# Feed-forward up projections: the high weights over both input halves as one matmul of 512 columns

## The chip, the cores and the metric

The kernel runs on one core of one Trainium2 chip. The metric is the device time of one execution in microseconds (us). The kernel before has a median of 1065.12 us over three runs (1064.92 to 1067.35).

## The reference

Three layers over 256 tokens of width 1024. The first two each have an attention mixer and, behind it, a feed-forward part; the third is a hybrid layer that the change doesn't touch. Everything is float32. The feed-forward part is:

```python
def conv_ffn(x, w_up, conv_w, conv_b, w_down):
    u = x @ w_up                                  # 1024 -> 2 * 2816
    up = jnp.pad(u, ((0, 0), (1, 1), (0, 0)))
    c = conv_b
    for j in range(3):
        c = c + conv_w[j] * up[:, j:j + s]        # three taps along the tokens
    g, val = c[..., :2816], c[..., 2816:]
    return (jax.nn.gelu(g) * val) @ w_down        # 2816 -> 1024
```

## The kernel before

**Products in two halves.** A float32 product is made of three matmuls in the type fp32r: each operand is split into a high half (a copy rounded to fp32r) and a low half (the value less the high half), and high x high, high x low and low x high are summed in PSUM (`mm3`, L397: L399 is weights high by input high, L400 weights high by input low, L401 weights low by input high). The input's halves are `xh` and `xl`, each eight blocks of 128 channels by 256 tokens. The weights come in chunks of 128 x 1024 into six slots `raw[0]` to `raw[5]`. ScalarE (ACT) makes `high` from `raw` (`split_high`, L357), and VectorE (DVE) or GpSimd (POOL) makes `low` (`split_low`, L368). In the feed-forward part GpSimd makes slot 3's and VectorE the others'. SyncE issues the load of the next chunk as soon as the slot's `low` is done.

**The feed-forward part** has 11 steps in each of two layers. A step has two halves, j = 0 and 1. A half takes 128 hidden channels: an up projection for the gate (slot and PSUM bank 2j) and one for the value (slot and bank 2j+1), each by `project_t` over eight blocks with three matmuls of 256 columns (24 matmuls), written to `W[bank][:, 0:TOK]` with TOK = 256; the other 256 columns of the bank are not used here. The down projection (slot 4+j) is 12 matmuls of 512 columns into `acc`. TensorE's order in a step (`ffn_pe`) is up(0, i), down(1, i-1), up(1, i), down(0, i); in the last step down(1, i-1) stands behind up(1, i).

**Between them**, for each half: ScalarE computes the middle tap and the bias of the gate from PSUM into `cg` (L1071), VectorE adds the two outer taps (L1118, L1121), the same for the value into `cv`, ScalarE applies GELU (L1077), GpSimd multiplies (`h`, L1156; the trace calls `h32` h), ScalarE copies the product's high half (`hh`, L1083) and GpSimd makes the low half (`hl`, L1158). Down needs both.

**What sets the order.** Each engine runs one hand-written list in order, and waits on semaphores in it. Per half ScalarE's list is: cg, high of the gate's slot, cv, high of the value's slot, GELU, (wait for h) hh, then one more high: slot 5 behind half 0, slot 4 behind half 1. VectorE's is: two taps on cg, low of the gate's slot, two taps on cv, low of the value's slot (GpSimd's for slot 3), with slot 5's low between the halves and slot 4's behind half 1. GpSimd's is: h, hl for half 0; h, hl, low of slot 3 for half 1. The first and the last step are written out, the nine between them are a loop. In the last step the highs and lows of half 1's slots stand later.

Of the kernel before, what the change touches and what calls it, by code (L numbers as in the profile page):

```python
# [23 lines left out]
P = 128  # L24
# [234 lines left out]
def build(nc, dram, y_out):  # L259
# [5 lines left out]
    def sb(name, shape, dt=F32):  # L265
        return scope[-1].enter_context(nc.sbuf_tensor(name, shape, dt))
# [28 lines left out]
    hid = sb("hid", [P, NT, D])  # L295
    hn = sb("hn", [P, NT, D])
    junk = sb("junk", [P, 512])
    xh = sb("xh", [P, KB, TOK], F32R)
    xl = sb("xl", [P, KB, TOK], F32R)
    stat = sb("stat", [P, 24])  # L300
    mean = sb("mean", [P, 16])

# [106 lines left out]
    def project_t(pe, out, k, width=P, offset=0, x=None, blocks=KB, arriving=None):  # L409


        x = x or (xh, xl)
        for b in range(blocks):
            if arriving is not None and b % 4 == 0:
                pe.wait_ge(n_["xl"], 4 * arriving + 2 + b // 2)
            o = b * width + offset
            last = mm3(pe, out, wslot(k, o, o + P), (x[0][:, b, :], x[1][:, b, :]), b == 0, b == blocks - 1)
        return last
# [602 lines left out]
    def ffn_pe(pe, layer):  # L1021
        p = (ph["ffn0"], ph["ffn1"])[layer]
        done = layer * FFN_STEPS

        def up(j, i):

            for gate, bank in ((1, 2 * j), (0, 2 * j + 1)):
                chunk_ready(pe, p, bank, i)
                if not (isinstance(i, int) and i + done == 0):
                    pe.wait_ge(f[j]["g_tap"] if gate else f[j]["v_tap"], 2 * (i + done))  # L1030
                first = isinstance(i, int) and i == 0 and j == 0 and gate
                project_t(pe, W[bank][:, 0:TOK], bank, arriving=2 * layer + 1 if first else None).then_inc(used[bank], 1)

        def down(j, i, start=False, stop=False):

            chunk_ready(pe, p, 4 + j, i)
            pe.wait_ge(f[j]["hl"], i + done + 1)
            rows_out(pe, 4 + j, hh[j], hl[j], start, stop).then_inc(used[4 + j], 1)

        def step(i):  # L1040
            last_step = isinstance(i, int) and i == FFN_STEPS - 1
            up(0, i)
            if not (isinstance(i, int) and i == 0) and not last_step:
                down(1, i - 1)
            up(1, i)
            if last_step:
                down(1, i - 1)
            down(0, i, start=isinstance(i, int) and i == 0)

        over(pe, FFN_STEPS, step)  # L1050
        seen = FFN_STEPS + done
        rows_out_end(pe, p, 5, 5, hh[1], hl[1], (f[1]["hh"], seen), (f[1]["hl"], seen))
# [6 lines left out]
    def ffn_act(act, layer):  # L1059
        p = (ph["ffn0"], ph["ffn1"])[layer]  # L1060
        done = layer * FFN_STEPS
        split = hi_of(act)

        def block(j, i, between):
            late = j == 1 and isinstance(i, int) and i == FFN_STEPS - 1
            for value in range(2):
                bank, s = 2 * j + value, f[j]
                act.wait_ge(used[bank], p.base[bank] + i + 1)
                if value and not (isinstance(i, int) and i + done == 0):
                    act.wait_ge(s["h32"], i + done)  # L1070
                act.activation((cg, cv)[value][j][:], W[bank][:, 0:TOK], ACT.Identity,  # L1071
                               scale=ffn_taps(layer, i, j, value, 1, 0),
                               bias=ffn_taps(layer, i, j, value, 3, 0)).then_inc((s["g_mid"], s["v_mid"])[value], 1)
                if not late:
                    refill(split, p, bank, i)
            act.wait_ge(f[j]["g_tap"], 2 * (i + done) + 2)
            act.activation(gelu[j][:], cg[j][:], ACT.Gelu_apprx_tanh).then_inc(f[j]["gelu"], 1)  # L1077
            if late:
                refill(split, p, 5, i - 1)
            act.wait_ge(f[j]["h32"], i + done + 1)  # L1080
            if not (isinstance(i, int) and i + done == 0):
                act.wait_ge(used[4 + j], used_before(i, j))
            act.activation(hh[j][:], h32[j][:], ACT.Copy).then_inc(f[j]["hh"], 1)  # L1083
            if late:
                for bank in (2 * j, 2 * j + 1):
                    refill(split, p, bank, i)
            between()

        def used_before(i, j):
            return p.base[4 + j] + i  # L1090

        def after_first(i):
            if not isinstance(i, int):
                refill(split, p, 5, i - 1)
            elif i == 0 and layer == 0:
                split(p, 5, 0)

        def step(i):
            if isinstance(i, int) and i == FFN_STEPS - 1:
                first_of_next(split, p)  # L1100
            block(0, i, lambda: after_first(i))
            block(1, i, lambda: refill(split, p, 4, i))

        over(act, FFN_STEPS, step)
        refill(split, p, 5, FFN_STEPS - 1)

    def ffn_dve(dve, layer):
        p = (ph["ffn0"], ph["ffn1"])[layer]
        done = layer * FFN_STEPS
        split = lo_of(dve)  # L1110

        def block(j, i):
            last_step = isinstance(i, int) and i == FFN_STEPS - 1
            for value in range(2):
                bank, s = 2 * j + value, f[j]
                mid, tap, c = (s["g_mid"], s["v_mid"])[value], (s["g_tap"], s["v_tap"])[value], (cg, cv)[value][j]
                dve.wait_ge(mid, i + done + 1)
                dve.scalar_tensor_tensor(c[:, 1:TOK], W[bank][:, 0:TOK - 1], ffn_taps(layer, i, j, value, 0, 0),  # L1118
                                         c[:, 1:TOK], ALU.mult, ALU.add).then_inc(tap, 1)
                dve.wait_ge(tap, 2 * (i + done) + 1)  # L1120
                dve.scalar_tensor_tensor(c[:, 0:TOK - 1], W[bank][:, 1:TOK], ffn_taps(layer, i, j, value, 2, 0),  # L1121
                                         c[:, 0:TOK - 1], ALU.mult, ALU.add).then_inc(tap, 1)
                if not (j and last_step):
                    refill(split, p, bank, i)

        def step(i):
            last_step = isinstance(i, int) and i == FFN_STEPS - 1
            block(0, i)
            if not isinstance(i, int):
                refill(split, p, 5, i - 1)  # L1130
            block(1, i)
            if isinstance(i, int) and i == 0:
                split(p, 5, 0)
            if last_step:
                refill(split, p, 5, i - 1)
                for bank in (2, 3):
                    refill(split, p, bank, i)
                first_of_next(split, p)
            if not (last_step and layer):
                refill(split, p, 4, i)  # L1140

        over(dve, FFN_STEPS, step)
        refill(split, p, 5, FFN_STEPS - 1)

    def ffn_pool(pool, layer):
        p = (ph["ffn0"], ph["ffn1"])[layer]
        done = layer * FFN_STEPS
        split = lo_of(pool, True)

        def hidden(j, i):  # L1150
            s = f[j]
            pool.wait_ge(s["gelu"], i + done + 1)
            pool.wait_ge(s["v_tap"], 2 * (i + done) + 2)
            if not (isinstance(i, int) and i + done == 0):
                pool.wait_ge(s["hh"], i + done)
            pool.tensor_tensor(h32[j][:], gelu[j][:], cv[j][:], ALU.mult).then_inc(s["h32"], 1)  # L1156
            pool.wait_ge(s["hh"], i + done + 1)
            pool.tensor_tensor(hl[j][:], h32[j][:], hh[j][:], ALU.subtract).then_inc(s["hl"], 1)  # L1158

        def step(i):  # L1160
            hidden(0, i)
            if not (isinstance(i, int) and i == 0):
                refill(split, p, 5, i - 1)
            refill(split, p, 0, i)
            refill(split, p, 1, i)
            hidden(1, i)
            refill(split, p, 2, i)
            refill(split, p, 3, i)
            refill(split, p, 4, i)
            if isinstance(i, int) and i == FFN_STEPS - 1:  # L1170
                first_of_next(split, p)

        over(pool, FFN_STEPS, step)
        refill(split, p, 5, FFN_STEPS - 1)
# [1514 lines left out]
    def att_pool(pool):  # L2689
# [14 lines left out]
        with pool.Fori(2, HEADS - 2) as r:  # L2704
# [3 lines left out]

    r_ = dict(tha=f[0]["g_mid"], thb=f[0]["v_mid"], mh=f[0]["hh"], ma=f[0]["g_tap"], mb=f[0]["v_tap"],
              sum=f[1]["g_tap"], ml=f[1]["v_tap"])  # L2710
    ACT_SEEN, DVE_SEEN = 2 * FFN_STEPS, 4 * FFN_STEPS
    tha, thb = sb("tha", [P, TOK]), sb("thb", [P, TOK])
    mga, mgb = sb("mga", [P, TOK]), sb("mgb", [P, TOK])
    mg = sb("mg", [P, TOK])
# [291 lines left out]
```

## Time and profile before

| | |
|---|---|
| median of three runs | 1065.12 us |
| the profiled execution's own time | 1066.56 us |
| its span, first to last instruction | 1064.8 us |
| mean granted TensorE clock | 0.997 |
| busy: TensorE / weight loads / VectorE / ScalarE / GpSimd | 1036.0 / 950.1 / 663.6 / 560.7 / 417.6 us |
| feed-forward part of layer 0, of layer 1 | about 128 to 312 us, 453 to 637 us |

The time around the span is 1.8 us. The matmuls of `mm3` are pipelined: a row shows each with its whole latency, so that the rows overlap, and what one costs is the distance between starts. Shares of busy time are averages over all stages; the feed-forward parts together are about a third of the span, and the sections below look at them alone.

### The profile page before, as it was taken

The page shows a single profiled execution, that of the slowest core. Times are in us where ns is not written, and L with a number is a line of the kernel's source. Part 1 is how long each engine was busy: PE and PEld are TensorE (multiplying, and loading weights), DVE is VectorE, ACT ScalarE, POOL GpSimd, SP SyncE. Part 2 cuts the span into 40 slices and gives each one's busy share as a digit, 9 for nine tenths or more (in the row PEclk, how much of TensorE's full clock was granted, in tenths as well). Part 3 has the DMA queues.
Part 4 walks back from the last instruction along what each step waited for, and adds up shares of the span by engine and source line. Part 5 has one row for each costly group of instructions (what it writes and reads, how often), then busy time and mean ns, then how long its engine had stood idle before and what let it go on. Part 6 is the DMA issues. An engine that isn't in the chain of part 4 may idle for free.

```text
span 1064.8 us, 21773 instructions
## 1 busy us (share of the span) xinstructions
PE 1036.0 (97%) x8216; PEld 950.1 (89%) x8216; DVE 663.6 (62%) x1074; ACT 560.7 (53%) x1022; POOL 417.6 (39%) x283
## 2 busy tenths in 40 slices
PE   9899999999999999999999999999999999999997
PEld 7799699999978998699999987899999899999996
DVE  4555767677665665776766755766676555554545
ACT  4555665555555555756555565644443355554433
POOL 1000234433351334334333463865653365534431
PEclk9999999999999999999999999999999999999999
DMA  8333465665543443365656434333213245546551
GB/s 317 120 124 128 132 218 186 195 197 178 177 159 130 140 147 131 114 225 183 205 184 201 159 102 148 110 120 109 92 61 120 80 133 149 155 137 209 199 181 43
DMA packets 46136, 162.27 MB, mean 152 GB/s; under 512 B 5248, under 2 KB 5504, under 8 KB 45952
## 3 DMA queue, kind: packets, MB, share of 16 engines
q1 hardware_dynamic: 44784, 156.78, 45.1%
q0 software_dynamic: 1296, 4.72, 1.4%
q8 instruction: 38, 0.62, 0.2%
q14 instruction: 18, 0.15, 0.0%
HBM read 160.43 MB, written 1.05 MB: 152 GB/s over the span
## 4 chain that ended last, share of the span: by engine, by line
PE 90%; DVE 3%; POOL 3%; ACT 2%; issue 1%; DMA 1%; DVEq 0%; SPq 0%; ACTq 0%
PE work L399 14%; PE work L401 14%; PE work L400 14%; PE work L1688 9%; PE acc L399 6%; PE acc L400 6%; PE acc L401 6%; PE work L2410 4%; PE work L2422 2%; PE acc L2422 2%; POOL low L368 1%; PE acc L1939 1%; PE acc L1953 1%; PE acc L1955 1%; POOL stat L559 1%
## 5 line engine op out<-in xcount | busy, mean ns | idle before, releaser
L368 POOL TENSOR_TENSOR low<-raw,high 128x1024 fp32r<-128x1024 f32 x109 | 265.7, 2441 | 293.4 <-ACT high L357 290.9
L368 DVE TENSOR_TENSOR low<-raw,high 128x1024 fp32r<-128x1024 f32 (+2 forms) x184 | 273.2, 1493 | 159.3 <-ACT high L357 159.2
L357 ACT ACTIVATE high<-raw 128x1024 fp32r<-128x1024 f32 (+2 forms) x293 | 299.5, 1032 | 43.9 <-DMA raw<-in_w_out 29.1
L399 PE MATMUL work<-xh,high 128*128 128x256 f32 (+1 forms) x1032 | 290.0, 281 | 0.7 <-DVE low L368 0.7
L400 PE MATMUL work<-xl,high 128*128 128x256 f32 (+1 forms) x1032 | 287.9, 279 | 0.0
L401 PE MATMUL work<-xh,low 128*128 128x256 f32 (+1 forms) x1032 | 287.8, 279 | 0.0
L399 PEld LDWEIGHTS work<-xh,high 128*128 128x128 f32 (+1 forms) x1032 | 193.2, 187 | 7.6 <-issue 4.8
L400 PEld LDWEIGHTS work<-xl,high 128*128 128x128 f32 (+1 forms) x1032 | 193.3, 187 | 2.0 <-issue 0.3
L401 PEld LDWEIGHTS work<-xh,low 128*128 128x128 f32 (+1 forms) x1032 | 193.3, 187 | 0.2
L1156 POOL TENSOR_TENSOR h<-gelu,cv 128x256 f32<-128x256 f32 x44 | 50.5, 1149 | 198.7 <-ACT gelu L1077 102.0
L1688 PE MATMUL work<-xh,high 128*128 128x256 f32 x256 | 76.7, 300 | 0.0
L1688 PE MATMUL work<-xl,high 128*128 128x256 f32 x256 | 71.7, 280 | 0.0
L1688 PE MATMUL work<-xh,low 128*128 128x256 f32 x256 | 71.4, 279 | 0.0
L399 PE MATMUL acc<-high,hh 128*128 128x512 f32 x168 | 65.9, 392 | 0.0
L400 PE MATMUL acc<-low,hh 128*128 128x512 f32 x168 | 65.8, 392 | 0.0
L401 PE MATMUL acc<-high,hl 128*128 128x512 f32 x168 | 65.4, 389 | 0.0
L1083 ACT ACTIVATE hh<-h 128x256 fp32r<-128x256 f32 x44 | 18.4, 418 | 77.7 <-POOL h L1156 77.7
L1688 PEld LDWEIGHTS work<-xh,high 128*128 128x128 f32 x256 | 48.1, 188 | 2.5
L1071 ACT ACTIVATE cv<-work,vec 128x256 f32<-128x256 f32 x44 | 24.8, 565 | 47.4 <-PE work L401 47.4
L1688 PEld LDWEIGHTS work<-xl,high 128*128 128x128 f32 x256 | 48.2, 188 | 0.0
L1688 PEld LDWEIGHTS work<-xh,low 128*128 128x128 f32 x256 | 48.1, 188 | 0.0
L1158 POOL TENSOR_TENSOR hl<-h,hh 128x256 fp32r<-128x256 f32 x44 | 34.1, 776 | 24.4 <-ACT hh L1083 24.4
(385 smaller groups left out, 2201.2 us busy)
## 6 DMA issues: line engine op xcount, KB each, us to landing
raw<-in_w_ffn SPq DMA_DIRECT2D x132, 512.0 KB, 4.3
raw<-in_w_out SPq DMA_DIRECT2D x39, 512.0 KB, 4.5
raw<-in_w_att SPq DMA_DIRECT2D x32, 512.0 KB, 3.7
raw<-in_w_diff SPq DMA_DIRECT2D x31, 512.0 KB, 4.3
raw<-in_w_gdn SPq DMA_DIRECT2D x24, 512.0 KB, 4.0
raw<-in_w_mla SPq DMA_DIRECT2D x8, 512.0 KB, 3.6
raw<-in_w_gdnz SPq DMA_DIRECT2D x8, 512.0 KB, 3.6
raw<-in_w_mla SPq DMA_DIRECT2D x8, 384.0 KB, 3.1
```

What stands on the lines that cost most here:

```text
L357: act.activation(high[k][:, 0:w], raw[k][:, 0:w], ACT.Copy).then_inc(high_done[k], 1)
L368: eng.tensor_tensor(low[k][:, 0:w], raw[k][:, 0:w], high[k][:, 0:w], ALU.subtract).then_inc(low_done[k], 1)
L399: pe.matmul(out, lhs[0], rhs[0], start=start, stop=False)
L400: pe.matmul(out, lhs[0], rhs[1], start=False, stop=False)
L401: return pe.matmul(out, lhs[1], rhs[0], start=False, stop=stop)
L1071: act.activation((cg, cv)[value][j][:], W[bank][:, 0:TOK], ACT.Identity, scale=ffn_taps(layer, i, j, value, 1, 0), bias=ffn_taps(layer, i, ...
L1083: act.activation(hh[j][:], h32[j][:], ACT.Copy).then_inc(f[j]["hh"], 1)
L1156: pool.tensor_tensor(h32[j][:], gelu[j][:], cv[j][:], ALU.mult).then_inc(s["h32"], 1)
L1158: pool.tensor_tensor(hl[j][:], h32[j][:], hh[j][:], ALU.subtract).then_inc(s["hl"], 1)
L1688: last = pe.matmul(W[x][:, 0:TOK], l[slot][:, b * P:(b + 1) * P], r[:, b, :], start=(s == 0), stop=(s == 23))
L2410: last = pe.matmul(W[0][:, t * TOK:(t + 1) * TOK], x[:, b, t * P:(t + 1) * P], w[k][:, o:o + TOK], start=(b == 0 and term == 0), stop=(b = ...
L2422: last = pe.matmul(out, w[k][:, b * P:(b + 1) * P], x[:, b, :], start=(s == 0), stop=(s == 23))
```

## The change

In the up projections the matmuls "weights high by input high" and "weights high by input low" become one matmul of 512 columns. Its moving operand is a view over both input halves, which now lie in one tensor, and it writes both halves of the PSUM bank: the first 256 columns hold high x high, to which the matmul of low weights still adds, and the last 256 hold high x low. So a block has two matmuls instead of three. The two sums are then added outside TensorE: ScalarE copies the second sum to SBUF (into `gelu` for the gate, `h32` for the value, which are free at that time) and VectorE adds it to the first in PSUM. Only then ScalarE computes the middle tap. The semaphores `g_tap` and `v_tap` count four events a step instead of two: copy, sum, and the two taps. Mixers, down projections and the hybrid layer keep their three matmuls.

```diff
-    xh = sb("xh", [P, KB, TOK], F32R)
-    xl = sb("xl", [P, KB, TOK], F32R)
+    x_both = sb("x_both", [P, 2, KB, TOK], F32R)
+    xh, xl = x_both[:, 0, :, :], x_both[:, 1, :, :]
...
+        def project_wide(bank, arriving):
+            out, both = W[bank][:, 0:TOK], W[bank][:].rearrange("p (a k) -> p a k", a=2)
+            for b in range(KB):
+                if arriving is not None and b % 4 == 0:
+                    pe.wait_ge(n_["xl"], 4 * arriving + 2 + b // 2)
+                h_, l_ = wslot(bank, b * P, (b + 1) * P)
+                if b == KB - 1:
+                    pe.matmul(out, l_, xh[:, b, :], start=False, stop=False)
+                last = pe.matmul(both, h_, x_both[:, :, b, :], start=(b == 0), stop=(b == KB - 1))
+                if b < KB - 1:
+                    pe.matmul(out, l_, xh[:, b, :], start=False, stop=False)
+            return last
...
-                    pe.wait_ge(f[j]["g_tap"] if gate else f[j]["v_tap"], 2 * (i + done))
+                    pe.wait_ge(f[j]["g_tap"] if gate else f[j]["v_tap"], 4 * (i + done))
-                project_t(pe, W[bank][:, 0:TOK], bank, arriving=2 * layer + 1 if first else None).then_inc(used[bank], 1)
+                project_wide(bank, 2 * layer + 1 if first else None).then_inc(used[bank], 1)
...
                 act.wait_ge(used[bank], p.base[bank] + i + 1)
+                if not (isinstance(i, int) and i + done == 0):
+                    act.wait_ge(s["hl"] if value else s["h32"], i + done)
+                act.activation((gelu, h32)[value][j][:], W[bank][:, TOK:2 * TOK],
+                               ACT.Copy).then_inc((s["g_tap"], s["v_tap"])[value], 1)
+                act.wait_ge((s["g_tap"], s["v_tap"])[value], 4 * (i + done) + 2)
...
-            act.wait_ge(f[j]["g_tap"], 2 * (i + done) + 2)
+            act.wait_ge(f[j]["g_tap"], 4 * (i + done) + 4)
...
+                dve.wait_ge(tap, 4 * (i + done) + 1)
+                dve.tensor_tensor(W[bank][:, 0:TOK], W[bank][:, 0:TOK], (gelu, h32)[value][j][:], ALU.add).then_inc(tap, 1)
                 dve.wait_ge(mid, i + done + 1)
...
-                dve.wait_ge(tap, 2 * (i + done) + 1)
+                dve.wait_ge(tap, 4 * (i + done) + 3)
...
-            pool.wait_ge(s["v_tap"], 2 * (i + done) + 2)
+            pool.wait_ge(s["v_tap"], 4 * (i + done) + 4)
```

The hybrid layer reuses these semaphores; the count from which it starts is raised to match.

## Rows read from the trace of the kernel before

**Rows 1.** The page, part 1: busy time of each engine, with its share and count

```profile
PE 1036.0 (97%) x8216; PEld 950.1 (89%) x8216; DVE 663.6 (62%) x1074; ACT 560.7 (53%) x1022; POOL 417.6 (39%) x283
```

**Rows 2.** Timeline of PE in one step: start us, us, what

```profile
209.25 0.28 PE L399 MATMUL work<-xh,high 128*128 128x256 f32 x1
...
214.86 0.39 PE L399 MATMUL acc<-high,hh 128*128 128x512 f32 x1
...
217.60 0.28 PE L399 MATMUL work<-xh,high 128*128 128x256 f32 x1
```

**Rows 3.** What PE waited for, longest in total: us, times, longest us

```profile
PE work L515 <- DVE hn L547: 4.3, 6, 1.9
```

**Rows 4.** Timeline of ACT, one round from hh to hh

```profile
161.29 0.42 ACT L1083 ACTIVATE hh<-h 128x256 fp32r<-128x256 f32 x1 [2.23 <-POOL h L1156]
161.62 1.04 ACT L357 ACTIVATE high<-raw 128x1024 fp32r<-128x1024 f32 x1
162.56 0.55 ACT L1071 ACTIVATE cg<-work,vec 128x256 f32<-128x256 f32 x1
163.01 1.05 ACT L357 ACTIVATE high<-raw 128x1024 fp32r<-128x1024 f32 x1
...
170.90 0.42 ACT L1083 ACTIVATE hh<-h 128x256 fp32r<-128x256 f32 x1 [3.46 <-POOL h L1156]
...
177.61 0.42 ACT L1083 ACTIVATE hh<-h 128x256 fp32r<-128x256 f32 x1 [2.23 <-POOL h L1156]
```

**Rows 5.** Timeline of DVE, the same round

```profile
162.69 3.28 DVE L368 TENSOR_TENSOR low<-raw,high 128x1024 fp32r<-128x1024 f32 x1 [2.31 <-ACT high L357]
165.89 0.47 DVE L1118 SCALAR_TENSOR_TENSOR cg<-work,vec,cg 128x255 f32<-128x255 f32 x1
166.51 0.48 DVE L1121 SCALAR_TENSOR_TENSOR cg<-work,vec,cg 128x255 f32<-128x255 f32 x1
166.91 1.21 DVE L368 TENSOR_TENSOR low<-raw,high 128x1024 fp32r<-128x1024 f32 x1
168.04 0.47 DVE L1118 SCALAR_TENSOR_TENSOR cv<-work,vec,cv 128x255 f32<-128x255 f32 x1
...
169.06 1.22 DVE L368 TENSOR_TENSOR low<-raw,high 128x1024 fp32r<-128x1024 f32 x1
172.30 1.23 DVE L368 TENSOR_TENSOR low<-raw,high 128x1024 fp32r<-128x1024 f32 x1 [2.03 <-ACT high L357]
...
176.22 0.48 DVE L1121 SCALAR_TENSOR_TENSOR cv<-work,vec,cv 128x255 f32<-128x255 f32 x1
```

**Rows 6.** Timeline of POOL, the same round

```profile
162.49 2.40 POOL L368 TENSOR_TENSOR low<-raw,high 128x1024 fp32r<-128x1024 f32 x1
169.22 1.65 POOL L1156 TENSOR_TENSOR h<-gelu,cv 128x256 f32<-128x256 f32 x1 [4.33 <-DVE cv L1121]
...
176.84 0.73 POOL L1156 TENSOR_TENSOR h<-gelu,cv 128x256 f32<-128x256 f32 x1 [4.70 <-issue]
```

**Rows 7.** Timeline of ACT: hh of half 1 in steps 0, 8, 9 of layer 0

```profile
144.94 0.42 ACT L1083 ACTIVATE hh<-h 128x256 fp32r<-128x256 f32 x1 [2.22 <-POOL h L1156]
...
276.35 0.42 ACT L1083 ACTIVATE hh<-h 128x256 fp32r<-128x256 f32 x1 [0.91 <-POOL h L1156]
...
293.04 0.42 ACT L1083 ACTIVATE hh<-h 128x256 fp32r<-128x256 f32 x1 [0.90 <-POOL h L1156]
```

**Rows 8.** The same in steps 0 and 9 of layer 1

```profile
469.00 0.42 ACT L1083 ACTIVATE hh<-h 128x256 fp32r<-128x256 f32 x1 [2.22 <-POOL h L1156]
...
618.04 0.42 ACT L1083 ACTIVATE hh<-h 128x256 fp32r<-128x256 f32 x1 [0.90 <-POOL h L1156]
```

**Rows 9.** Groups of DVE by line and form: busy us, mean ns, idle before

```profile
L1898 DVE TENSOR_TENSOR work<-work,const 64x256 f32<-64x256 f32 x8 | 3.5, 434 | 1.4 <-ACT mt L1815 1.3
```

**Rows 10.** Timeline of POOL: the first scalar step behind each layer's feed-forward part

```profile
313.07 0.56 POOL L601 TENSOR_TENSOR stat<-mean,vec 128x1 f32<-128x1 f32 x1
...
639.42 0.56 POOL L601 TENSOR_TENSOR stat<-mean,vec 128x1 f32<-128x1 f32 x1
```

More of the change, by code:

```diff
@@ L2710, in build @@
               sum=f[1]["g_tap"], ml=f[1]["v_tap"])
-    ACT_SEEN, DVE_SEEN = 2 * FFN_STEPS, 4 * FFN_STEPS
+    ACT_SEEN, DVE_SEEN = 2 * FFN_STEPS, 8 * FFN_STEPS
     tha, thb = sb("tha", [P, TOK]), sb("thb", [P, TOK])
```

## The prediction

> **What bounds the kernel now.** I read the page's busy times first, then TensorE's starts inside one feed-forward step, then what TensorE waited for, and last the lists of the other three engines over one step. TensorE is busy 97% of the span and VectorE 62%, ScalarE 53%, GpSimd 39% [rows 1]. That alone says that TensorE's work is the time, and that the rest has room. Both hold only on average, so the feed-forward step has to be read for itself.
>
> *TensorE's step.* Between 209.25 and 214.86 lie two up projections, 48 matmuls of 256 columns: 5.61 us, 0.117 us each. Between 214.86 and 217.60 lies one down projection, 12 of 512 columns: 2.74 us, 0.228 us each [rows 2]. A step has two of either: 2 x (5.61 + 2.74) = 16.70 us. Inside the feed-forward parts TensorE waits for nobody: its longest waits of all are for `hn`, between the parts, 1.9 us at most [rows 3].
>
> *The round of the other engines.* This is the view that decides. In the second and third step they do not wait for TensorE, because they are a little late, so their list shows its own length. From `hh` of half 1 at 161.29 to the next at 177.61 the round takes 16.32 us [rows 4], only 0.38 us less than TensorE's step. Followed piece by piece, one engine works and the others wait: ScalarE's hh and high of slot 4; VectorE's low of slot 4 from 162.69, which lasts 3.28 us and not 1.22 because GpSimd's low of slot 3 started at 162.49 and ran until 164.89 [rows 5, 6]; then taps (165.89, 166.51), low (166.91), taps (168.04), low (169.06); GpSimd's h at 169.22, whose 1.65 us again lies partly behind VectorE's low; hh at 170.90, a high, VectorE's low (172.30), taps, low, taps until 176.70; h at 176.84; hh at 177.61 [rows 4 to 6]. VectorE's tap follows its own previous low at once: the middle tap `cg` was computed by ScalarE long before, at 162.56, while VectorE was in its low [rows 4, 5]. Later in the part the round has caught up and TensorE sets the pace: hh at 276.35 and 293.04, 16.69 us apart [rows 7]. So two loops of nearly equal length run side by side.
>
> **The change, part by part.**
>
> *TensorE.* A block had 3 x 0.117 = 0.351 us and gets 0.228 + 0.117 = 0.345 us, at the pace of [rows 2]; one matmul of 512 columns is hardly shorter than two of 256. With 32 blocks a step that is 16.52 us, 0.18 less; over 22 steps 3.9 us. This is all that the change can bring. (For the 512-column matmul over two separate regions of SBUF there is no row. If the second region cost nothing it is the above; if it cost as much as the two matmuls that it replaces, the gain is zero.)
>
> *ScalarE's copy.* 88 copies of 128x256 from PSUM. The nearest row is `cg` itself, 0.55 us [rows 4]. It goes in front of `cg`, where ScalarE waits for TensorE or VectorE anyway. While VectorE does taps and a low (over 2 us), ScalarE does one high of 1.05 us [rows 4], then the next copy. I cost the copies at nothing. Their cover is VectorE's list; without it each would cost 0.4 to 0.55 us.
>
> *VectorE's add, and the two waits.* Here is the price. VectorE's list for a bank was: tap, tap, low. It becomes: add, wait for `cg`, tap, tap, low. `cg` may only start when the add is done, so it can no longer be computed behind VectorE's previous low: VectorE stands still while ScalarE computes it, and what is queued behind it, the taps and the low of the next chunk, moves by as much. A round trip per bank costs
> - the add: 0.43 us (256 columns from PSUM and SBUF to PSUM: [rows 9]; the taps with 255 columns take 0.47 [rows 5]);
> - VectorE to ScalarE: 0.04 us, as GpSimd to ScalarE (h ends at 176.84 + 0.73 = 177.57, hh starts at 177.61 [rows 4, 6]);
> - `cg`: 0.56 us [rows 4];
> - ScalarE back to VectorE: 0.04 us.
>
> Together 1.07 us, four times a step: 4.28 us. None of it has cover, since [rows 4 to 6] show that every piece of the round waits for the one before. GELU adds 0.05 us: ScalarE reaches it behind high, about when the taps end. The rest of the round keeps its shape: the low of slot 3 on GpSimd still starts 0.2 us ahead of slot 4's on VectorE, and hits it as before; the new adds meet no work of GpSimd. The round becomes 16.32 + 4.28 + 0.05 = 20.65 us.
>
> So TensorE, with 16.52 us of work, is no longer the bound. It will wait in each step: laid out from these numbers, about 3.5 us for `hl` of half 0 in front of down(0), 0.6 us in front of down(1). The loads gain room, and I cost them at nothing: they are issued when a low is done, and a step is 4 us longer.
>
> For the add alone the Trainium skill has a price (VectorE: DVE Perf Modes, "The TRN2 errata"): with a PSUM source 120 cycles and one per element at 0.96 GHz, here 0.39 us. By it the sum would be about 3 us lower; the row above goes by what was measured here.
>
> *The sum.* From hh of half 1 in step 0 to that in step 9 there are nine rounds: 9 x 20.65 = 185.9 us. Before it was 293.04 - 144.94 = 148.1 us in layer 0 [rows 7] and 618.04 - 469.00 = 149.0 us in layer 1 [rows 8]. That is +37.8 and +36.9. The first step: two round trips lie fully behind each other, of the first two a part lies behind TensorE; laid out in the same way, hh of half 1 comes 3.3 us later in layer 0 and 3.6 us in layer 1. The last step: four round trips (4.3 us), less what the engines had waited for TensorE there. I follow it to GpSimd's first scalar step of the norm, at 313.07 and 639.42 [rows 10], which waits for GpSimd's last low and not for TensorE: +1.8 and +2.8 us. All together 37.8 + 36.9 + 3.3 + 3.6 + 1.8 + 2.8 = 86 us. The profiled execution took 1066.56 us, 1.4 us above the median of 1065.12; against it 1152.8, against the median **1151 us**.
>
> *The bounds.* Round trip: with the shortest add and `cg` that these rows allow (0.38 and 0.50) and no handing over it is 0.9 us; with 0.47 for the add and 0.1 us more at each hand-over, since in the loop two dependent taps start 0.62 us apart although one takes 0.47 [rows 5], it is 1.3 us. Over 88 banks that is 15 us less or 20 us more. Hence 1136 to 1171 within this case.
>
> **The rivals.**
>
> *TensorE stays the bound: faster.* If the round has slack that I don't see, for instance because `cg` lets VectorE go on with the next low first, the four round trips vanish and only TensorE's 3.9 us are left: 1061 us. The point at which it decides is the length of the round: it must stay under 16.52 us, and before it had 16.32, so only 0.2 us is free for four round trips. For it speaks the average load of VectorE and ScalarE [rows 1]; against it that the hand-written list puts the wait ahead of taps and low. Chance 0.04.
>
> *Half-hidden: no change.* The round trips cost just what the 0.38 us of slack and TensorE's gain hold, about 0.15 us each, if add and `cg` ran nearly side by side. Time 1062 to 1068. The waits forbid it. Chance 0.03.
>
> *TensorE's clock falls.* The granted clock was full, with waits of at most 1.9 us [rows 3]; the new wait of 3.5 us in each step is longer than any of them. If the clock fell to the lower level behind every such wait and stayed there, TensorE's step would take twice 16.52 us, 33 us, against a round of 20.65: 22 x 12.4 = 270 us more, some 1420 us. If it only stayed for a few microseconds, TensorE would lose less than the 4 us that it waits anyway, and the time stays. Chance of the bad form 0.05.
> The Trainium skill says that idleness brings the clock down (TensorE: Matmul & The Clock Gate, Part 1: the array runs at 1.2 GHz by default and activity releases it to 2.4 GHz). No row here has it lowered inside a feed-forward part.
>
> *The collision moves away.* If VectorE's low of slot 4 came ahead of GpSimd's low of slot 3, it would take 1.22 instead of 3.28 us and the round 18.6 us: about 1108 us. The order hangs on 0.2 us [rows 5, 6], but both start from the same `hh`. Chance 0.04.
>
> **How the numbers follow.** The likeliest case, a round of about 20.65 us, has 0.84. The range of 8 in 10 cuts its thin ends: 1138 to 1169 us. What a measurement of this kernel can tell from no change is 0.3%, 3 us. Faster by more than that: 0.04; within it: 0.03; slower: 0.93.
>
> **What would show it.** Right: hh of half 1 lies 20 to 21.3 us apart in both layers; VectorE idles about 0.65 us in front of each first tap, released by `cg`; TensorE waits for `hl` in each step, longest near 3.5 us, and its busy share falls to about 90%; pairs of matmuls start 0.345 us apart; the chain that ended last runs through add, cg, tap and low and no longer through matmuls alone. Wrong: a distance of 16.5 us between those `hh`, the copies rather than the adds on the chain, or a granted clock well under 0.99.

## The result, and the profile after

The kernel with the change takes 1170.13 us (median of four runs, 1169.61 to 1170.45) against 1065.69 us before: a ratio of 1.0977, with a 95% interval of 1.0958 to 1.0996. It is slower, as forecast, but by 104 us and not by 86: the time lies 1 us above the range of 1138 to 1169.

The page after, parts 1 and 2 of the changed kernel (against [rows 1]):

```profile
PE 1075.9 (92%) x7512; PEld 943.0 (81%) x7512; DVE 699.6 (60%) x1162; ACT 586.8 (50%) x1110; POOL 413.1 (35%) x283
...
PEclk9999989898899999999888899899999999999999
```

TensorE's busy time has grown, although 704 matmuls are gone, and the granted clock has dips in the two feed-forward parts. ScalarE and VectorE have got 26 and 36 us more work, in 103 us more span, so their busy shares have even fallen. Part 4 of the page gives the chain of work that ended last. Before, it was nearly all TensorE:

```profile
PE 90%; DVE 3%; POOL 3%; ACT 2%; issue 1%; DMA 1%; DVEq 0%; SPq 0%; ACTq 0%
```

In the changed kernel it is a mixture:

```profile
PE 53%; DVE 15%; ACT 13%; issue 11%; POOL 6%; ACTq 1%; DVEq 1%; POOLq 0%
ACT high L357 8%; PE work L1709 8%; DVE low L368 7%; PE work L399 6%; PE work L401 5%; PE work L400 5%; POOL h L1177 4%; PE work L2431 4%; DVE work L1137 3%; PE work L2443 2%; PE acc L399 2%; PE acc L401 2%; PE acc L400 2%; ACT cg L1090 2%; DVE cg L1139 2%
```

The round of the other engines, seen as in [rows 4 to 6], one round after the change. ScalarE:

```profile
213.52 0.42 ACT L1102 ACTIVATE hh<-h 128x256 fp32r<-128x256 f32 x1 [0.90 <-POOL h L1177]
...
218.79 0.56 ACT L1090 ACTIVATE cg<-work,vec 128x256 f32<-128x256 f32 x1 [3.63 <-DVE work L1137]
...
222.28 0.56 ACT L1090 ACTIVATE cv<-work,vec 128x256 f32<-128x256 f32 x1 [1.71 <-DVE work L1137]
...
229.07 0.56 ACT L1090 ACTIVATE cg<-work,vec 128x256 f32<-128x256 f32 x1 [1.60 <-DVE work L1137]
...
232.54 0.57 ACT L1090 ACTIVATE cv<-work,vec 128x256 f32<-128x256 f32 x1 [1.69 <-DVE work L1137]
...
235.27 0.42 ACT L1102 ACTIVATE hh<-h 128x256 fp32r<-128x256 f32 x1 [0.90 <-POOL h L1177]
```

VectorE in the same round:

```profile
214.93 3.28 DVE L368 TENSOR_TENSOR low<-raw,high 128x1024 fp32r<-128x1024 f32 x1 [2.31 <-ACT high L357]
218.13 0.42 DVE L1137 TENSOR_TENSOR work<-work,gelu 128x256 f32<-128x256 f32 x1
219.52 0.48 DVE L1139 SCALAR_TENSOR_TENSOR cg<-work,vec,cg 128x255 f32<-128x255 f32 x1 [0.97 <-ACT cg L1090]
...
221.68 0.42 DVE L1137 TENSOR_TENSOR work<-work,h 128x256 f32<-128x256 f32 x1
222.99 0.48 DVE L1139 SCALAR_TENSOR_TENSOR cv<-work,vec,cv 128x255 f32<-128x255 f32 x1 [0.89 <-ACT cv L1090]
...
227.24 1.23 DVE L368 TENSOR_TENSOR low<-raw,high 128x1024 fp32r<-128x1024 f32 x1 [2.01 <-ACT high L357]
228.38 0.43 DVE L1137 TENSOR_TENSOR work<-work,gelu 128x256 f32<-128x256 f32 x1
229.78 0.48 DVE L1139 SCALAR_TENSOR_TENSOR cg<-work,vec,cg 128x255 f32<-128x255 f32 x1 [0.98 <-ACT cg L1090]
...
231.94 0.42 DVE L1137 TENSOR_TENSOR work<-work,h 128x256 f32<-128x256 f32 x1
233.25 0.48 DVE L1139 SCALAR_TENSOR_TENSOR cv<-work,vec,cv 128x255 f32<-128x255 f32 x1 [0.89 <-ACT cv L1090]
```

And GpSimd:

```profile
214.72 2.41 POOL L368 TENSOR_TENSOR low<-raw,high 128x1024 fp32r<-128x1024 f32 x1
224.33 1.48 POOL L1177 TENSOR_TENSOR h<-gelu,cv 128x256 f32<-128x256 f32 x1 [7.21 <-DVE cv L1142]
...
234.49 0.74 POOL L1177 TENSOR_TENSOR h<-gelu,cv 128x256 f32<-128x256 f32 x1 [7.43 <-ACT gelu L1096]
```

From hh at 213.52 to the next at 235.27 the round takes 21.75 us; it was 16.32. In front of each first tap VectorE now stands idle for 0.89 to 0.98 us "<-ACT cg" or cv, and ScalarE in front of each of its own for 1.6 to 3.6 us "<-DVE work": each waits for the other. VectorE's low of 3.28 us next to GpSimd's of 2.41 is as before.

What TensorE waited for in the changed kernel (us in total, times, longest), against [rows 3]:

```profile
PE acc L399 <- POOL hl L1179: 60.7, 23, 3.8
```

In the looped steps this is one wait a step, in front of down(0); the forecast second one, of 0.6 us in front of down(1), doesn't appear. Behind the wait TensorE drops in most steps for a few microseconds to the lower of its two clock levels, 1.2 instead of 2.4 GHz: the matmuls of the down projection then start 0.43 us apart and not 0.23.

```profile
227.21 0.47 PE L399 MATMUL acc<-high,hh 128*128 128x512 f32 x1 [1.98 <-POOL hl L1179]
...
229.89 0.63 PE L399 MATMUL acc<-high,hh 128*128 128x512 f32 x1
230.32 0.63 PE L400 MATMUL acc<-low,hh 128*128 128x512 f32 x1
```

### The profile page after: what moved, and what is told of

It is laid out like the page before. It is cut to its first block, busy times and chain, and to the rows that moved or that the text cites. A ratio compares the mean times of both kernels' runs of the same rounds, so it can differ in the third digit from the quotient of the medians.

```text
span 1168.2 us, 20661 instructions
## 1 busy us (share of the span) xinstructions
PE 1075.9 (92%) x7512; PEld 943.0 (81%) x7512; DVE 699.6 (60%) x1162; ACT 586.8 (50%) x1110; POOL 413.1 (35%) x283
## 3 DMA queue, kind: packets, MB, share of 16 engines
HBM read 160.43 MB, written 1.05 MB: 138 GB/s over the span
## 4 chain that ended last, share of the span: by engine, by line
PE 53%; DVE 15%; ACT 13%; issue 11%; POOL 6%; ACTq 1%; DVEq 1%; POOLq 0%
ACT high L357 8%; PE work L1709 8%; DVE low L368 7%; PE work L399 6%; PE work L401 5%; PE work L400 5%; POOL h L1177 4%; PE work L2431 4%; DVE work L1137 3%; PE work L2443 2%; PE acc L399 2%; PE acc L401 2%; PE acc L400 2%; ACT cg L1090 2%; DVE cg L1139 2%
## 5 line engine op out<-in xcount | busy, mean ns | idle before, releaser
L1034 PE MATMUL work<-x_both,high 128*128 128x512 f32 x704 | 248.0, 396 | 0.4 <-POOL low L368 0.4
L1036 PE MATMUL work<-x_both,low 128*128 128x256 f32 x616 | 173.6, 282 | 0.0
L1034 PEld LDWEIGHTS work<-x_both,high 128*128 128x128 f32 x704 | 130.5, 190 | 27.1 <-issue 1.6
L1036 PEld LDWEIGHTS work<-x_both,low 128*128 128x128 f32 x616 | 117.4, 191 | 4.2
L399 PEld LDWEIGHTS acc<-high,hh 128*128 128x128 f32 x168 | 37.7, 224 | 75.1 <-issue 68.0
L1709 PE MATMUL work<-x_both,high 128*128 128x256 f32 x512 | 97.4, 290 | 0.0
L399 PE MATMUL work<-x_both,high 128*128 128x256 f32 (+1 forms) x328 | 93.1, 284 | 0.7 <-DVE low L368 0.7
L400 PE MATMUL work<-x_both,high 128*128 128x256 f32 (+1 forms) x328 | 91.6, 279 | 0.0
L401 PE MATMUL work<-x_both,low 128*128 128x256 f32 (+1 forms) x328 | 91.5, 279 | 0.0
L1709 PEld LDWEIGHTS work<-x_both,high 128*128 128x128 f32 x512 | 77.7, 188 | 2.5
L1709 PE MATMUL work<-x_both,low 128*128 128x256 f32 x256 | 71.4, 279 | 0.0
L399 PEld LDWEIGHTS work<-x_both,high 128*128 128x128 f32 (+1 forms) x328 | 60.9, 186 | 4.9 <-issue 3.5
L400 PEld LDWEIGHTS work<-x_both,high 128*128 128x128 f32 (+1 forms) x328 | 60.9, 186 | 0.2
L401 PEld LDWEIGHTS work<-x_both,low 128*128 128x128 f32 (+1 forms) x328 | 60.9, 186 | 0.2
```

The lines of the kernel that those rows point to most:

```text
L399: pe.matmul(out, lhs[0], rhs[0], start=start, stop=False)
L400: pe.matmul(out, lhs[0], rhs[1], start=False, stop=False)
L401: return pe.matmul(out, lhs[1], rhs[0], start=False, stop=stop)
L1034: last = pe.matmul(both, h_, x_both[:, :, b, :], start=(b == 0), stop=(b == KB - 1))
L1036: pe.matmul(out, l_, xh[:, b, :], start=False, stop=False)
L1709: last = pe.matmul(W[x][:, 0:TOK], l[slot][:, b * P:(b + 1) * P], r[:, b, :], start=(s == 0), stop=(s == 23))
```

## The experiments

All ratios are to the kernel before on the same chip.

**1. TensorE's part alone** (`wide_alone`). The 512-column matmuls without copy and add; the product of high weights and low input is left out.

```diff
 kernel before, with x_both and project_wide of the change
-project_t(pe, W[bank][:, 0:TOK], bank, ...)
+project_wide(bank, ...)          # columns 256 to 511 of the bank are not read
```

> TensorE's part of the change alone: the 512-column matmuls as in the change, but neither copy nor add, so the product of high weights and low input is left out of the up projections. Theory (the round of the other engines costs the time, the wide matmul saves 0.18 us a step): round 16.3 us, TensorE's step 16.52 us, 1061 us, with a granted clock as before. Rival (the wide matmul over two regions, or a lowered clock, costs time by itself): over 1066 us, matmul pairs more than 0.351 us apart.

Measured: 1065.02 us, ratio 0.9992 (0.9983 to 1.0001). The matmuls do no harm, and bring nothing that can be told from noise; the 1061 us that I expected did not come. TensorE's timeline in this kernel:

```profile
275.05 0.40 PE L1034 MATMUL work<-x_both,high 128*128 128x512 f32 x1
275.29 0.28 PE L1036 MATMUL work<-x_both,low 128*128 128x256 f32 x1
275.41 0.40 PE L1034 MATMUL work<-x_both,high 128*128 128x512 f32 x1
...
280.64 0.40 PE L399 MATMUL acc<-high,hh 128*128 128x512 f32 x1
...
283.40 0.40 PE L1034 MATMUL work<-x_both,high 128*128 128x512 f32 x1
```

One block starts 0.35 us after the other, just as with three matmuls of 256 columns (5.61 us for 16 blocks [rows 2], here 275.05 to 280.64 = 5.59). The wide one takes 0.23 to 0.24 us, twice a narrow one. The 0.02 us less in the up projections comes back in the down projection behind them, 2.76 us (280.64 to 283.40) instead of 2.74: half a step, two up projections and one down, takes 8.35 us here (275.05 to 283.40) and took 8.35 us before (209.25 to 217.60 [rows 2]). So TensorE's step is not shorter at all, and there was nothing to win instead of 3.9 us.

**2. The add stays, the wait goes** (`add_after_mid`). ScalarE computes cg before the add, so that the middle tap lacks the second sum.

```diff
-                act.wait_ge((s["g_tap"], s["v_tap"])[value], 4 * (i + done) + 2)
...
+                dve.wait_ge(mid, i + done + 1)
                 dve.wait_ge(tap, 4 * (i + done) + 1)
                 dve.tensor_tensor(W[bank][:, 0:TOK], W[bank][:, 0:TOK], (gelu, h32)[value][j][:], ALU.add).then_inc(tap, 1)
-                dve.wait_ge(mid, i + done + 1)
+                dve.wait_ge(tap, 4 * (i + done) + 2)
```

> Copy and add stay, but ScalarE no longer waits for the add: the middle tap is computed from the first sum alone (so the middle tap lacks the product of high weights and low input), and VectorE adds behind it. Theory (VectorE's standing still while ScalarE computes cg is most of the price): a bank costs the add and one dependent start, about 0.6 us instead of 1.36, the round falls from 21.75 to about 18.7 us, 1105 us. Rival (the volume of added work is the price, whoever waits): 1165 to 1170 us.

Measured: 1107.7 us, ratio 1.0392 (1.0376 to 1.0407). Timeline of VectorE in it:

```profile
213.79 1.23 DVE L368 TENSOR_TENSOR low<-raw,high 128x1024 fp32r<-128x1024 f32 x1 [2.02 <-ACT high L357]
214.94 0.43 DVE L1137 TENSOR_TENSOR work<-work,gelu 128x256 f32<-128x256 f32 x1
215.51 0.48 DVE L1139 SCALAR_TENSOR_TENSOR cg<-work,vec,cg 128x255 f32<-128x255 f32 x1
```

Low to tap is 1.72 us (213.79 to 215.51) instead of 2.54 in the changed kernel (227.24 to 229.78). The round is 18.65 us. All of the added work is still there, and three fifths of the loss are gone (1170 to 1108 of 1170 to 1066): the price is mostly waiting. The rest is the add standing in VectorE's list: add to tap is 0.57 us (214.94 to 215.51), four times a round 2.3 us, and the round is 18.65 - 16.32 = 2.3 us longer than before the change.

**3. Three matmuls, with the side work** (`side_work_three`). Blocks 1 to 6 of each up projection take three matmuls again; copy and add stay.

```diff
-                last = pe.matmul(both, h_, x_both[:, :, b, :], start=(b == 0), stop=(b == KB - 1))
+                if b in (0, KB - 1):
+                    last = pe.matmul(both, h_, x_both[:, :, b, :], start=(b == 0), stop=(b == KB - 1))
+                else:
+                    pe.matmul(out, h_, xh[:, b, :], start=False, stop=False)
+                    pe.matmul(W[bank][:, TOK:2 * TOK], h_, xl[:, b, :], start=False, stop=False)
```

> The change with three matmuls again for blocks 1 to 6 of each up projection (high x low goes to the other half of the bank as in the change); the side work is untouched. Theory (TensorE is off the path in the steps): round 21.75 us, the same time as the change within 0.3%, 1168 to 1173 us. Rival (TensorE with its lowered clock still counts): its work is 2% more, and the time is 5 us or more above the change.

Measured: 1170.24 us, ratio 1.0981 (1.0964 to 1.0998), the same as the change. TensorE is off the path. (By experiment 1 these matmuls take no more time than the wide ones, so this run says less than it was meant to: only that how TensorE gets the second sum plays no part. Experiment 5 asks more.)

**4. The loop written out** (`flat_after`, and `flat_before` as its control). The nine looped steps are nine copies, with constants in waits and addresses; each engine's order stays.

```diff
-        over(act, FFN_STEPS, step)      # likewise pe, dve, pool
+        over_flat(act, FFN_STEPS, step)
```

> The change with the nine looped steps written out, so that no wait or address stands in a register. Theory (in the loop a wait in front of an instruction with an address in a register is an instruction of its own, and that makes a hand-over 0.16 to 0.25 us instead of 0.04): round trip 1.07 us, the two taps 0.52 instead of 0.62 us apart, round 20.2 us, 1143 us. Rival (the long hand-over belongs to an add that writes PSUM): round 21.3 us, 1162 us.

> The kernel before with the nine looped steps written out: the control for the written-out change. Theory (before the change TensorE sets the step, 16.7 us, so shorter hand-overs bring nothing): 1065 us, within 0.3% of before. Rival (writing out helps or hurts by itself, through fetching the instructions for instance): more than 5 us to either side, and then the 24 us that writing out brought to the change are not all its round's.

Measured: `flat_after` 1146.61 us, ratio 1.0754 (1.0737 to 1.0770), 24 us below the change; `flat_before` 1065.35 us, 0.9995 (0.9986 to 1.0005). So writing out doesn't change the time by itself. VectorE's timeline in `flat_after`:

```profile
213.39 0.42 DVE L1141 TENSOR_TENSOR work<-work,gelu 128x256 f32<-128x256 f32 x1
214.44 0.48 DVE L1143 SCALAR_TENSOR_TENSOR cg<-work,vec,cg 128x255 f32<-128x255 f32 x1 [0.63 <-ACT cg L1094]
214.96 0.48 DVE L1146 SCALAR_TENSOR_TENSOR cg<-work,vec,cg 128x255 f32<-128x255 f32 x1
```

And ScalarE's, between the first two of these:

```profile
213.84 0.56 ACT L1094 ACTIVATE cg<-work,vec 128x256 f32<-128x256 f32 x1 [3.40 <-DVE work L1141]
```

The add ends at 213.81, cg starts at 213.84 and ends at 214.40, the tap starts at 214.44: the round trip is 1.05 us, with hand-overs of 0.03 and 0.04. In the changed kernel's loop the add ends at 218.13 + 0.42 = 218.55, cg starts at 218.79 and ends at 219.35, the tap starts at 219.52: 1.39 us, with 0.24 and 0.17; for the value it is 1.31. The add itself takes 0.42 in both, and writes PSUM in both, so the long hand-over doesn't belong to the add. The chain that ended last shows what stands in the hand-over (ACTq is ScalarE's sequencer). In the loop, for the gate of half 0 and for its value:

```profile
218.13 0.43 DVE work L1137
...
218.58 0.08 ACTq L1090
...
218.69 0.04 ACTq L1090
...
218.79 0.57 ACT cg L1090
```

```profile
222.13 0.08 ACTq L1090
222.21 0.07 issue
```

In `flat_after` the same view has nothing of ScalarE's sequencer between the add and cg. In the loop there is an instruction of its own of 0.08 us, which begins when the add has ended, and for this gate a second one of 0.04 us: the hand-over is 0.24 us with two of them and 0.18 with one. What of the first is the wait and what the address in a register was not taken apart, as the run takes away both.

Two taps also come closer, 0.52 instead of 0.62 us apart, and the round is 20.40 us: 1.35 less. The four round trips give 1.2 of that and the four pairs of taps 0.4; about 0.25 is lost again, most of it in front of GpSimd's h of half 1. In the loop GELU and the last tap end together there; written out GELU ends 0.2 us behind the tap, and h waits for it.

**5. Filling TensorE's wait** (`filled`). Sixteen more wide matmuls in each step; their results are overwritten.

```diff
+                if j and gate:
+                    for _ in range(16):
+                        pe.matmul(W[bank][:].rearrange("p (a k) -> p a k", a=2), high[bank][:, 0:P],
+                                  x_both[:, :, 0, :], start=True, stop=True)
                 project_wide(bank, 2 * layer + 1 if first else None).then_inc(used[bank], 1)
```

> The change with 16 more 512-column matmuls (3.7 us) in front of each up projection of half 1's gate; their results are overwritten. They fill the time in which TensorE waited. Theory (the round is 21.75 us whatever TensorE does, and its lowered clock of 0.963 costs nothing but a little at the ends of the parts): clock at 0.99 or above, 1167 to 1172 us. Rival (the lowered clock costs time in each step): clock up and the time below 1160 us.

Measured: 1170.5 us, ratio 1.0978 (1.0960 to 1.0997); mean clock 0.995. One round of either kernel by stretches: its length, the busy time (and count) of TensorE, its weight loads, VectorE, ScalarE and GpSimd, then the granted clock, DMA share and GB/s. The changed kernel:

```profile
215.30:237.00 21.70, 19.72 (x98) 16.60 (x97) 13.08 (x18) 10.47 (x18) 6.01 (x6) 0.92 0.47 145
```

And `filled`:

```profile
215.30:237.00 21.70, 20.92 (x104) 17.29 (x104) 13.12 (x17) 10.42 (x19) 6.00 (x6) 1.00 0.45 145
```

(A step of the changed kernel has 88 matmuls, one of `filled` 104. TensorE's steps don't start with these stretches, so the changed kernel's counts vary, 98 here.) 3.7 us more of matmuls in each step cost nothing, and the clock at its full 1.00 instead of 0.92 wins nothing. In the looped steps the lowered clock is a consequence of the wait, and it is paid from the wait.

**6. Highs earlier in ScalarE's list** (`early_high`). The high of slots 5 and 4 goes ahead of the wait for h.

```diff
             act.activation(gelu[j][:], cg[j][:], ACT.Gelu_apprx_tanh).then_inc(f[j]["gelu"], 1)
             if late:
                 refill(split, p, 5, i - 1)
+            else:
+                between()
             act.wait_ge(f[j]["h32"], i + done + 1)
...
-            between()
+                between()                # inside "if late:"
```

> The change with one move in ScalarE's list: the high of slots 5 and 4 is made ahead of its wait for h and not behind hh. VectorE's low of that slot can then start about 2 us earlier, twice a round. Theory (any piece taken from the serial round shortens the step until TensorE's 16.7 us): round between 17 and 18.5 us, 1075 to 1110 us. Rival (only the new add and wait matter, or the low is late for another reason): above 1150 us.

Measured: 1083.66 us, ratio 1.0166 (1.0149 to 1.0183). The round is 17.3 us, 4.4 less. A move that touches neither the add nor its wait takes back 86 of the 104 us. This says what bounds the changed kernel: the serial round as a whole.

The move does two things, though. The lows start earlier, and the collision of the two lows moves: VectorE's low of slot 4 now comes ahead of GpSimd's low of slot 3 and takes 1.23 us instead of 3.28, while the next low takes 1.71 instead of 1.22.

```profile
215.86 1.23 DVE L368 TENSOR_TENSOR low<-raw,high 128x1024 fp32r<-128x1024 f32 x1 [0.98 <-ACT high L357]
...
219.43 1.71 DVE L368 TENSOR_TENSOR low<-raw,high 128x1024 fp32r<-128x1024 f32 x1
```

```profile
217.64 2.41 POOL L368 TENSOR_TENSOR low<-raw,high 128x1024 fp32r<-128x1024 f32 x1
```

That alone is 2.05 - 0.49 = 1.6 of the 4.4 us. It is the mechanism of the rival "the collision moves away", brought on here by another edit.

**7. And the add earlier in VectorE's list** (`early_both`). The add of a bank goes ahead of the low in front of its taps.

```diff
 order of VectorE in a step (k is the bank; add, two taps, low of a slot)
-add 0, taps 0, low 0, add 1, taps 1, low 1, low 5, add 2, taps 2, low 2, add 3, taps 3, low 4
+add 0, low 4 (of the step before), taps 0, add 1, low 0, taps 1, low 1, add 2, low 5, taps 2, add 3, low 2, taps 3
```

> As early_high, and in VectorE's list the add of a bank goes ahead of the low that stands in front of the bank's taps, so that ScalarE computes cg while VectorE makes that low, as before the change. All the change's work is still done. Theory: the four waits of about 0.95 us are covered again, the round is shorter than TensorE's step, which sets the pace with 16.7 us: 1064 to 1070 us. Rival (copy and add as such slow the step, by their volume or at PSUM): 1085 us or more.

Measured: 1070.3 us, ratio 1.0040 (1.0026 to 1.0054). VectorE in this kernel:

```profile
221.81 0.43 DVE L1137 TENSOR_TENSOR work<-work,gelu 128x256 f32<-128x256 f32 x1 [1.34 <-ACT gelu L1085]
222.15 1.25 DVE L368 TENSOR_TENSOR low<-raw,high 128x1024 fp32r<-128x1024 f32 x1
223.33 0.47 DVE L1144 SCALAR_TENSOR_TENSOR cg<-work,vec,cg 128x255 f32<-128x255 f32 x1
```

That is 0.3 us above the 1064 to 1070 that I expected, and far under the rival's 1085. Between low and tap there is no idle time left: cg was computed during the low. Steps are 16.68 us apart, TensorE's own pace. With all 88 copies and 88 adds the looped steps are as long as TensorE makes them before the change (16.69). What is left, 4.3 us, lies at the ends of the parts: hh of half 1 in the last step of layer 1 comes at 637.22 instead of 632.87, with 2.4 us more between the end of layer 0's part and the first of these hh in layer 1, and about 1.5 us more in layer 1's last step. That wasn't taken apart further.

**8. The same move before the change** (`before_early_high`).

> The kernel before with the same move of ScalarE's highs as in early_high. Theory (before the change TensorE sets the step in the looped part, so a shorter round brings nothing there): 1065 us, within 0.3% of before. Rival (the round still held the time of before somewhere, at the first steps for instance): 3 us or more faster.

Measured: 1066.56 us, ratio 1.0006 (0.9997 to 1.0015). As expected: hh of half 1 is 16.69 us apart from the second looped step on, TensorE's pace. No version beat the kernel before clear of noise: with TensorE's step as long with wide matmuls as without, there was nothing to win.

## Why the prediction was right, and where it was wrong

The mechanism came as forecast: four uncovered round trips a step make the serial round the bound. The time didn't, because one term of the sum was too small, the hand-over between VectorE and ScalarE.

*What bounds before.* Right: a serial round of 16.3 us next to TensorE's 16.7. `flat_before` shortens the round (15.9 us in its first looped steps, until TensorE sets 16.69) and wins nothing, nor does `before_early_high`; `early_high` shortens it after the change and wins 86 us.

*TensorE's gain.* Mis-sized, 3.9 us against nothing. I put the pace of down projections, 0.228 us, on the wide matmul; next to narrow ones it takes 0.233, and the pair comes out at 0.35 us like three narrow ones: the case that the prediction put in brackets, a gain of zero. It had no weight in the sum, since TensorE no longer sets the step.

*The copies.* Right: 0.37 us each, covered. `early_both` has all of them in a step of 16.68 us.

*The add.* Right: 0.43 forecast, 0.42 measured. The Trainium skill's price for a PSUM source (VectorE: DVE Perf Modes, "The TRN2 errata") gives an estimate of 0.39 us, a little short of the 0.42 measured; its column is for an output in SBUF, and this add writes PSUM.

*The round trip.* This is the step that failed: "VectorE to ScalarE: 0.04 us, as GpSimd to ScalarE", and the same back. In half 0 the hand-overs are 0.24 and 0.17 us for the gate, 0.18 and 0.15 for the value, and half 1 is alike. VectorE's idle time in front of the first taps was forecast as 0.65 us and is 0.89 to 0.98. The round trips add 1.39 + 1.31 + 1.40 + 1.31 = 5.41 us and not 4.28, and 16.32 + 5.41 is the measured round of 21.75 to 0.02 us (the 0.05 that I gave GELU isn't needed). I had given 20 to 21.3 us for the distance of two hh as the sign of being right, and it lies above. I had taken the 0.04 from `hh`, whose addresses are constant. The price of the instruction that actually stands behind the new wait was in the rows, in the two taps 0.62 us apart with 0.47 of work; I used it for the bound and not for the value. `flat_after` confirms the rest of the trip: with hand-overs of 0.03 and 0.04 it is 1.05 us, against my 1.07.

*The sum by its terms*, from the same points as in the prediction. hh of half 1 in steps 0 and 9 of layer 0, then of layer 1, and GpSimd's first scalar step behind each part, in the changed kernel (against [rows 7, 8, 10]):

```profile
148.02 0.42 ACT L1102 ACTIVATE hh<-h 128x256 fp32r<-128x256 f32 x1 [1.54 <-POOL h L1177]
...
343.99 0.42 ACT L1102 ACTIVATE hh<-h 128x256 fp32r<-128x256 f32 x1 [0.90 <-POOL h L1177]
...
525.55 0.42 ACT L1102 ACTIVATE hh<-h 128x256 fp32r<-128x256 f32 x1 [1.54 <-POOL h L1177]
...
720.46 0.42 ACT L1102 ACTIVATE hh<-h 128x256 fp32r<-128x256 f32 x1 [0.90 <-POOL h L1177]
```

```profile
365.42 0.56 POOL L601 TENSOR_TENSOR stat<-mean,vec 128x1 f32<-128x1 f32 x1
...
744.13 0.56 POOL L601 TENSOR_TENSOR stat<-mean,vec 128x1 f32<-128x1 f32 x1
```

| term | forecast | measured |
|---|---|---|
| nine rounds, layer 0 | +37.8 | 343.99 - 148.02 - 148.10 = +47.9 |
| nine rounds, layer 1 | +36.9 | 720.46 - 525.55 - 149.04 = +45.9 |
| first step, layer 0 | +3.3 | 148.02 - 144.94 = +3.1 |
| first step, layer 1 | +3.6 | (525.55 - 469.00) - (365.42 - 313.07) = +4.2 |
| last step, layer 0 | +1.8 | (365.42 - 343.99) - (313.07 - 293.04) = +1.4 |
| last step, layer 1 | +2.8 | (744.13 - 720.46) - (639.42 - 618.04) = +2.3 |
| sum | +86 | +105 |

The two lines of rounds miss 19 us, all of the error. (The profiled executions are 1170.06 - 1066.56 = 103.5 us apart; what stands behind the last of these points was 1.3 us shorter in the one of the changed kernel.)

Behind layer 0's part the lowered clock does cost a little: the twelve matmuls of the last down projection take from 361.05 to 365.57, 4.5 us, where the pace of [rows 2] makes it 2.7. Of these 1.8 us about 0.5 reach what follows: the first two scalar steps of the norm are 2.08 us apart (365.42 to 367.50) and were 1.62 apart before. In `side_work_three`, where the same matmuls take 3.1 us, they are 1.62 apart too. `filled`, whose extra matmuls lie elsewhere, has the slow matmuls as well, and 2.09.

*The range.* The bounds of the case reached to 1171, from just such a hand-over; I cut the end off to 1169 as thin. It wasn't thin: it was the value that the nearest row gave (0.43 + 0.15 + 0.56 + 0.15 = 1.29 us a trip, 1170 us).

*The rivals.* TensorE as the bound, and no change: excluded. The clock: the benign form came. The new wait, 3.8 us at the longest, did bring TensorE to its lower level for a part of most steps, and in them that took from the wait alone; `filled` shows it. By the Trainium skill (TensorE: Matmul & The Clock Gate, Part 1) idleness lowers the clock, and the trace agrees: 0.92 and 0.84 in most looped steps, 1.00 where the wait is filled. The prediction named a granted clock well under 0.99 as a sign of being wrong; the mean is 0.963 in the changed kernel and 0.995 in `filled`, at the same time, so here the clock was no sign of what bounds. The collision of the two lows stayed in the changed kernel, at 3.28 us.

## What to carry to other kernels

Before adding a hand-over between two engines, measure the round of all the engines that hand work to each other, not their busy shares: here VectorE at 62% and ScalarE at 53% had 0.4 us free in a step of 16.7. A producer that is asked for just when its consumer is ready costs its whole time on the path; where its input is handed over earlier, in front of other work of the consumer, it cost nothing in the looped steps (`early_both`). Take the price of a hand-over from a row with the same kind of instruction behind the same kind of wait, in a loop if the new one is in a loop.

## What the runs showed of the hardware that I had not expected

- A hand-over between VectorE and ScalarE took 0.03 to 0.04 us where wait and address are constants, and 0.14 to 0.26 us in the loop, where the wait stands as an instruction of its own in front of one whose address is in a register. Four round trips are 5.41 us in the loop and 4 x 1.05 written out, 1.2 us less in a round.
- In the up projections a matmul of 512 columns takes as long as two of 256 (0.233 against 2 x 0.117 us). Loading the weights once less for each block didn't shorten half a step: 8.35 us with either.
- TensorE at its lower clock in parts of most steps, a mean of 0.963, cost next to nothing here: 1170.1 us, and 1170.5 us with the clock at 0.995. About 0.5 us of it shows, behind layer 0's part.
